# A two-layer encoder trunk on one core: weights and low parts ahead of copies and squares in the first unit, head-norm fans in pairs, and one value ahead of two maxima

## The reference, cut to what matters

```
x = x + 0.5 * swiglu(rmsnorm(x), w_gate, w_up, w_down)      # 1024 -> 2816 -> 1024
h = rmsnorm(x)
layer 0:  z = h @ w_in                       # u, g, q, k, v and 8 forget logits
          a = silu(rmsnorm(conv31(u * sigmoid(g)) + b))     # depthwise, 31 taps
          q, k = rmsnorm per head of 64; o = softmax(q k^T / 8 + decay, causal) @ v
          x = x + concat(a, o) @ w_out
layer 1:  x = x + (gate_b * conv3(gate_c * hh)) @ w_out
x = x + 0.5 * swiglu(rmsnorm(x), ...)
```

## Time and profile before

| | us |
|---|---|
| median of 3 runs | 1849.33 (1849.28 to 1849.39) |
| the profiled execution, its own time | 1849.31 |
| its span in the trace | 1847.5 |
| TensorE busy | 1835.4 |
| VectorE busy | 824.3 |
| ScalarE busy | 633.2 |
| GpSimd busy | 356.7 |

### The profile page before, as it was taken

How to read it: one execution, slowest core, us unless ns; L and a number is a source line. 1 busy time by engine, 2 the same in 40 slices (tenths; PEclk the granted TensorE clock), 3 DMA queues, 4 the chain that set the end, 5 groups by cost and what they waited for, 6 DMA issues and landing times.

```text
span 1847.5 us, 22267 instructions
## 1 busy us (share of the span) xinstructions
PE 1835.4 (99%) x8269; PEld 1504.5 (81%) x8269; DVE 824.3 (45%) x934; ACT 633.2 (34%) x833; POOL 356.7 (19%) x295
## 2 busy tenths in 40 slices
PE   8999999999999999999999999999999999999999
PEld 7888888888668888888888888888888888888887
DVE  6343433368856443443344343333455544343321
ACT  5333322247765333332233333222212333333221
POOL 5111111129853111111111111011213221111000
PEclk9999999999999999999999999999999999999999
DMA  5333343233104333333323333432333333333331
GB/s 162 103 91 102 91 125 94 77 80 92 35 24 126 101 93 98 95 114 105 88 79 95 99 93 100 121 94 81 92 91 103 91 102 92 102 91 110 108 111 35
DMA packets 341403, 174.85 MB, mean 95 GB/s; under 512 B 6304, under 2 KB 340332, under 8 KB 341356
## 3 DMA queue, kind: packets, MB, share of 16 engines
q1 hardware_dynamic: 337100, 172.12, 32.2%
q10 hardware_dynamic: 4256, 2.11, 0.4%
HBM read 172.10 MB, written 2.10 MB: 94 GB/s over the span
## 4 chain that ended last, share of the span: by engine, by line
PE 93%; DVE 4%; ACT 2%; issue 1%; POOL 0%; ACTq 0%; DVEq 0%; POOLq 0%
PE bank L1324 30%; PE bank L1326 30%; PE bank L1325 30%; DVE w_lo L964 1%; DVE conv L1000 1%; ACT w_hi L645 1%; ACT tap_prod L804 0%; PE bank L1530 0%; DVE neg_max L1180 0%; PE bank L1546 0%; ACT probs_a L857 0%; PE bank L1465 0%; DVE k_n L1129 0%; PE bank L1515 0%; DVE q_n L1129 0%
## 5 line engine op out<-in xcount | busy, mean ns | idle before, releaser
L964 DVE TENSOR_TENSOR w_lo<-raw,w_hi 128x1024 fp32r<-128x1024 f32 (+2 forms) x308 | 408.5, 1327 | 697.0 <-ACT w_hi L645 696.5
L1324 PE MATMUL bank<-xg_hi,w_hi 128*128 128x512 f32 x1728 | 673.8, 390 | 2.7 <-DVE w_lo L964 2.6
L1326 PE MATMUL bank<-xg_hi,w_lo 128*128 128x512 f32 x1728 | 672.3, 389 | 0.0
L1325 PE MATMUL bank<-xg_lo,w_hi 128*128 128x512 f32 x1728 | 672.3, 389 | 0.0
L645 ACT ACTIVATE w_hi<-raw 128x1024 fp32r<-128x1024 f32 (+2 forms) x308 | 339.9, 1104 | 775.6 <-PE bank L1326 775.5
L1324 PEld LDWEIGHTS bank<-xg_hi,w_hi 128*128 128x128 f32 x1728 | 324.3, 188 | 72.7 <-DVE w_lo L964 3.1
L1326 PEld LDWEIGHTS bank<-xg_hi,w_lo 128*128 128x128 f32 x1728 | 324.3, 188 | 67.6
L1325 PEld LDWEIGHTS bank<-xg_lo,w_hi 128*128 128x128 f32 x1728 | 324.4, 188 | 66.9 <-issue 0.2
L545 POOL TENSOR_TENSOR scaled<-acted,rstd 128x512 f32<-128x512 f32 x92 | 118.8, 1291 | 835.9 <-ACT acted L722 787.9
L1324 PE MATMUL bank<-h_hi,w_hi 128*128 128x512 f32 x704 | 274.5, 390 | 0.0
L1326 PE MATMUL bank<-h_hi,w_lo 128*128 128x512 f32 x704 | 274.0, 389 | 0.0
(11 more groups left out here) (193 smaller groups left out, 991.9 us busy)
## 6 DMA issues: line engine op xcount, KB each, us to landing
raw<-in_ffn_w_gate SPq DMA_DIRECT2D x88, 512.0 KB, 3.8
raw<-in_ffn_w_up SPq DMA_DIRECT2D x88, 512.0 KB, 3.8
raw<-in_ffn_w_down SPq DMA_DIRECT2D x64, 704.0 KB, 4.5
raw<-in_od_w_in SPq DMA_DIRECT2D x24, 512.0 KB, 3.7
raw<-in_ev_w_in SPq DMA_DIRECT2D x20, 512.0 KB, 3.8
raw<-in_ev_w_out SPq DMA_DIRECT2D x16, 256.0 KB, 2.8
raw<-in_od_w_out SPq DMA_DIRECT2D x8, 512.0 KB, 3.9
x_rows<-in_x SPq DMA_DIRECT2D x4, 512.0 KB, 6.7
```

The source lines that it names most:

```text
L964: dve.tensor_tensor(w_lo[:, u % 2, c0:c0 + n], raw[:, u % 4, 0:n], raws(w_hi[:, u % 2, c0:c0 + n]), ALU.subtract).then_inc(wlo_ready, 1)
L1324: pe.matmul(dst, a[0], b[0], start=start, stop=False)
L1325: pe.matmul(dst, a[0], b[1], start=False, stop=False)
L1326: return pe.matmul(dst, a[1], b[0], start=False, stop=stop)
```

## The change

Three things. In the first unit VectorE makes the low parts of tiles 0 and 1 and the low part of the weights before it copies the tiles, and tiles are copied in the order 0, 1, 2, 5, 6, 7, 3, 4. ScalarE makes the high part of the weights ahead of the first square, and six of the eight squares follow the second weights. The sum over partitions moves from the end of unit 1 into the middle of unit 2, and units 1 to 3 wait for the copies out of their banks. In the phase `v` the four fans stand in two pairs. On VectorE the taps around them are dealt out otherwise, four go into the attention steps 3 to 6, and the last value stands ahead of the maxima of step 1.

```diff
+    COPIES = [0, 1, 2, 5, 6, 7, 3, 4]
-    TAPS_V, TAPS_T = [2, 2, 2, 2, 2, 3, 4], 0
+    TAPS_V, TAPS_T = [2, 2, 3, 3, 3], 1
-    QK_FANS, V_SUMS, V_FANS = {6: 0, 7: 2}, (0, 0), [(1, 2), (1, 3), (2, 0), (2, 1)]
+    QK_FANS, V_SUMS, V_FANS = {6: 0, 7: 2}, (0, 0), {(1, 2): AB, (2, 0): AB + 2}
...
+            def first_square(n):
+                act.wait_ge(x_new, n + 1)
+                if n >= 2:
+                    act.wait_ge(sq_added, n - 1)
+                act.activation(sq[:, n % 2, :], x[:, COPIES[n], :], ACT.Square).then_inc(sq_ready, 1)
...
             for j in (0, 1):
                 first_high(j)
+            split_hi(phases[0], 0, 0)
             first_square(0)
-            split_hi(phases[0], 0, 0)
             for j in (2, 3):
                 first_high(j)
+            first_square(1)
             for j in range(4, KD):
-                first_square(j - 3)
                 first_high(j)
             split_hi(phases[0], 0, 1)
-            for j in (KD - 3, KD - 2, KD - 1):
+            for j in range(2, KD):
                 first_square(j)
...
                 qk_scale(4)
+                qk_scale(5)
                 conv_taps(TAPS_V[2])
-                qk_scale(5)
-                conv_taps(TAPS_V[3])
                 split_lo(ph, 0, 3)
                 qk_scale(6)
-                conv_taps(TAPS_V[4])
                 qk_scale(7)
-                conv_taps(TAPS_V[5])
+                conv_taps(TAPS_V[3])
...
                         value(1)
-                        conv_taps(TAPS_V[6])
+                        conv_taps(TAPS_V[4])
+                        value(3)
                         maxima(1)
-                        value(3)
...
-                    if t >= 2:
+                    if t >= 3:
                         conv_taps(TAPS_T, late=t >= LAST_IN_BANK)
...
             for j in (0, 1):
                 first_low(j)
+            split_lo(phases[0], 0, 0)
+            for j in (0, 1):
                 first_copy(j)
-            split_lo(phases[0], 0, 0)
-            for j in range(2, KD):
+            for j in (2, 3):
                 first_low(j)
-                if 3 <= j < KD - 1:
-                    first_copy(j - 1)
+            first_copy(2)
+            for j in range(4, KD):
+                first_low(j)
+            first_copy(3)
             split_lo(phases[0], 0, 1)
-            for j in (KD - 2, KD - 1):
-                first_copy(j)
+            for n in range(4, KD):
+                first_copy(n)
...
+                        if first and ph is phases[0] and u:
+                            pe.wait_ge(x_new, u + 3)
+                        if first and ph is phases[0] and u in (0, 2):
+                            hook = late_squares if u else turn_in
                         projection(ph, g, u, wait_x=first and u == 0, before=hook)
...
                         if first and u == 1 and ph is phases[0]:
-                            sum_squares(ph)
...
+            def late_squares(k):
+                if k == KD // 2:
+                    sum_squares(phases[0])
...
                             elif (u, tb) in V_FANS:
-                                fan(AB + V_FANS.index((u, tb)))
+                                fan(V_FANS[u, tb])
+                                fan(V_FANS[u, tb] + 1)
```

More of the change, by code:

```diff
@@ L663, in first_high @@
                                scale=vec[:, j + GAIN_COL[0]:j + GAIN_COL[0] + 1]).then_inc(xhi_ready, 1)
-            def first_square(j):
-                act.wait_ge(x_new, j + 1)
-                if j >= 2:
-                    act.wait_ge(sq_added, j - 1)
-                act.activation(sq[:, j % 2, :], x[:, j, :], ACT.Square).then_inc(sq_ready, 1)
+            def first_square(n):
[3 more added lines that the diff above has]
+                act.activation(sq[:, n % 2, :], x[:, COPIES[n], :], ACT.Square).then_inc(sq_ready, 1)
             logs = [0]
@@ L1240, in first_low, with first_copy @@
                                          ALU.mult, ALU.subtract).then_inc(xlo_ready, 1)
-            def first_copy(j):
+            def first_copy(n):
+                j = COPIES[n]
                 dve.tensor_copy(x[:, j, :], bank[TURN_BANKS[j % len(TURN_BANKS)]][:, :]).then_inc(x_new, 1)
@@ L1360, in group @@
                         hook = None
-                        if first and ph is phases[0] and u == 0:
-                            hook = turn_in
+                        if first and ph is phases[0] and u:
+                            pe.wait_ge(x_new, u + 3)
+                        if first and ph is phases[0] and u in (0, 2):
+                            hook = late_squares if u else turn_in
                         projection(ph, g, u, wait_x=first and u == 0, before=hook)
```

## The result

The changed kernel takes **1852.65 us** (median of 15 runs, 1851.31 to 1853.82); beside it on the same chip the kernel before takes 1849.32 us (15 runs, 1849.27 to 1849.39). The ratio is 1.0018, 95% interval 1.0011 to 1.0025: 3.3 us slower. The forecast was 1850.6 with a range up to 1852.6, so it missed by 2.05 us and the median lies just outside the range.

What follows compares the result with a forecast made beforehand. TensorE was taken as the bound, busy 1835.4 of 1847.5 us at full clock. First units +2.2 and attention -0.9 gave +1.3 us on the 1849.33 median: 1850.6 us, range 1848.5 to 1852.6.

Steps and rivals of the forecast that it cites:

- The gain of the first unit: First units: TensorE's first product at 9.8 instead of 11.38, unit 1 at 18.4 against 19.83, 1.4 us ahead.
- The stand at unit 2: Unit 2: squares paced by GpSimd's adds hold the third `w_hi`; TensorE stands 3.0 us, starting at 27.05 against 26.35.
- The rest of the first units at full clock: Units 2 to 5: later sum makes the fifth `w_lo` late, waits 0.45 and 0.2 us; first units +2.2 us.
- the bounds given: First units: the +2.2 us term could lie between +0.8 and +2.7 us.
- rival (c): Unit 2: the 3.0 us stand drops TensorE's clock to half; 1852.6, or 1854 if twice as long; 12 in 100.
- a clock under full behind the stand: After the stand at unit 2: a granted clock under full would show the forecast wrong.
- the wait for the odd probabilities: Attention near 500: TensorE waits about 1.4 us for the odd probabilities.
- GpSimd's bound on the turn: First attention turn: GpSimd scales the odd head until 501.62, so third scores start at 502.2 against 503.09, -0.9 us.
- Attention at full clock: Attention input: scores start about 1.8 us earlier, but only -0.9 us is kept; range 0 to -2.2.
- the taps moved into steps 3 to 6: Attention steps 3 to 6: four taps cost TensorE nothing if they fit VectorE's waits; otherwise the gain is 0.2.
- The fans: Attention input: a pair takes 0.43 us like a lone fan, so pairing saves 0.86 us.
- The sum: Whole kernel: first units +2.2 and attention -0.9 make +1.3 us, forecast 1850.6 us.

Runs made afterwards that it cites:

- e4: Changed kernel with ten filler matmuls that nothing reads on TensorE ahead of unit 2; 1852.18 us.
- e1: Changed kernel with the attention input put back as before, so only the first units changed; 1853.03 us.
- e3: Changed kernel with ScalarE making unit 2's high weights after four squares instead of eight; 1851.56 us.
- e2: Changed kernel with the first units put back as before, so only the attention input changed; 1849.67 us.
- e5: e2 with six filler matmuls between the even and odd half of the first attention turn; 1848.75 us.
- e9: e6 with VectorE's tap of step 6 moved ahead of the last value copy; 1848.26 us.
- e6: e2 with two more of GpSimd's tap adds moved behind the first scalings of odd heads; 1848.71 us.
- e11: Kernel before with only the four last fans of the head norms issued in two pairs; 1849.34 us.
- e8: e7 with GpSimd freed as in e6, the third square before the last high part, unit 2's weights after six squares; 1847.85 us.
- e10: e8 with the tap of step 6 moved ahead of the last value copy as in e9; 1847.40 us.
- e12: First-units part of the change alone, with three mends (third square earlier, unit 2's high weights before last two squares, selectors later); 1848.47 us.
- e7: e3 with GpSimd building its selectors behind the first phase's gates instead of ahead of them; 1849.79 us.

## Why the prediction was right and wrong

**The gain of the first unit: right.** First product 9.80 for 9.8, unit 1 at 18.35 for 18.4.

**The stand at unit 2: right**, place, cause and size: 27.08 for 27.05, six squares behind the second `w_hi` paced by adds, last square at 24.10 for 24.2, stand 2.86 us for 3.0 (27.05 less 23.95 is 3.1). One of the two meetings of an add and a `w_lo` held the squares, the other none of what unit 2 needs.

**The rest of the first units at full clock: nearly right.** e4 shows it without the fall at unit 2: the fifth `w_lo` was to be ready at 39.4 (by the forecast's own terms 30.8 + 9.64 - 0.9 it is 39.5) and TensorE to wait 0.45; TensorE starts at 39.50 after 0.35. The term was +2.2 us; e1's lower group gives +2.6, within the bounds given. The missing 0.4 comes a little at a time: e4's units 4, 5 and 6 start at 39.50, 45.21 and 50.79, against 37.34, 42.78 and 48.22 before, which is 2.16, 2.43 and 2.57 us behind, and the forecast had 2.0 at unit 4 and 2.2 from unit 5 on.

**The clock: the step that failed.** I had this fall as rival (c), with its mechanism, place and price, and gave it 12 in 100. I reasoned that "the longest stand inside the rows of before is 1.70 us, and no slice shows less than the full 2.4 GHz", which says nothing of a stand of 3.0 us; and the slices could not have shown a fall, since the changed kernel's, with two falls, show the same forty 9s. So the sum held nothing for the clock, and a clock under full behind the stand, which I had named as a sign of being wrong, came. By e1's groups the fall happened in 8 of its 11 runs. Rival (c)'s 1852.6 is the measured median to 0.05 us by luck: it put 2 us for one fall on top of 1850.6, while the median run, with a mean clock of 0.999, lost about 1.2 us by one fall and 0.8 us more than forecast in order. A fall costs less than I worked out for two reasons. Half rate lasted 3.4 us (28.3 to 31.7) and not 4; the start of the kernel, from which I took the 4 us, shows 1.00 in the clock column although its turns took twice as long, so it was no measured fall of the clock. And of the 1.7 us of lost work not all arrives. The sum of squares starts at 31.30 instead of e4's 29.92, 1.38 us late, and `mean_sq` behind it at 32.57 instead of 30.98, 1.59 late; but the fifth `w_lo` takes 1.54 us instead of e4's 1.89, and unit 4, which waits for it in both, starts 1.24 us late. e3 shows the other case: its three upper runs lie 1.7 us over the middle ones, the whole of the lost work.

**The second fall: missed.** I forecast the wait for the odd probabilities, about 1.4 us, and put nothing for it beyond GpSimd's bound on the turn. It is a 1.87 us stand, only 0.17 us more than the 1.70 us of the earlier trace rows behind which the profiled run of the kernel before shows full clock, and it drops the clock in 7 of e2's 11 runs. The 0.45 us that it is longer are a mis-sized term: a lone fan costs TensorE more than the 0.43 us to the next product, because the steps ahead of it and behind that product are longer too, 0.31 and 0.34 us for 0.23. TensorE's timeline before:

```profile
482.19 0.39 PE L1326 MATMUL bank<-w_hi,xg_lo 128*128 128x512 f32 x1
482.50 0.50 PE L1585 MATMUL bank<-head_rows,fan_rows 4*128 4x512 f32 x1
482.93 0.50 PE L1324 MATMUL bank<-w_hi,xg_hi 128*128 128x512 f32 x1
483.27 0.39 PE L1325 MATMUL bank<-w_lo,xg_hi 128*128 128x512 f32 x1
```

Two fans fewer to stand alone gave 1.3 us and not 0.86: e2's first scores start at 490.65, without a wait, where TensorE would have come at 491.97 before and at 491.1 by the forecast.

The Trainium skill, "TensorE: Matmul & The Clock Gate", section "Why this matters for your kernels", warns of gaps over about 3 us; for the first stand (2.86) the measurement is about at that edge, and for stands of 1.87 and 1.90 us it goes further than the page: behind them the clock fell too, in 7 of 11 and 3 of 11 runs. Where the two differ, the measurement decides.

**Attention at full clock: right in kind, too large.** Forecast -0.9, measured -0.5. The third scores of e5 start at 502.30 for the forecast 502.2: that lead was there, and still is at the ninth (516.22 for 517.02). It is lost at turn 6 (tenth scores 519.28 for 519.21), and 0.5 us of it comes back at the turn near 524, where the kernel before waits 0.45 us. The step that failed reads that the taps moved into steps 3 to 6 "cost nothing on TensorE as long as they fit in waits that VectorE has there", with 0.2 as the gain if one does not. One does not, the one in step 6; e9 moves it and gets 0.5 us more. I had looked at VectorE's room as a sum and not at step 6, where a weight split stands. That the price was 1.66 us on the maximum and not the tap's own 0.7 comes from two neighbours made longer (1.45 for 0.67, 1.17 for 0.69) when shifted: in e6 GpSimd's square starts at 513.67, ahead of the `w_lo` (513.80), in e9 at 513.64, behind it (513.15). By the Trainium skill, "SBUF — State Buffer", section "SBUF: two separate sides", the one that starts first holds the shared ports; the trace agrees (1.45 against 0.67). Durations of this kind, 2.18 for 1.22, I had used at the first units and not here.

**The fans: right in kind and worth nothing alone.** 0.43 us for a pair, but more saved by it than forecast, as above; e11 shows no gain in time, because the last `k_n` bounds the scores.

**The sum.** Forecast +2.2 - 0.9 = +1.3. Measured at full clock +2.6 - 0.5 = +2.1, with the clock's falls +3.3 in the median. So 0.8 us of the miss are sizes (0.4 in the first units, 0.4 in attention) and 1.2 us are the clock. In which of the three groups the median of 15 runs lies is chance; from the 1.000 group alone the forecast is 0.7 us off.

**What stays open.** Why a fall comes in one run and not in the next of the same kernel. The run's mean clock says that it did, nothing in the profile of one run says why. Why the fall at unit 5 of e3 costs 1.7 us rests on its groups and one profile. e4's run of 1854.2 us and the two high runs of e5 are not explained. Whether the stand of 1.70 us can drop the clock too is only hinted at: of the 113 timed runs of the kernel before 7 took 1850.16 to 1850.30 us, 0.9 over the rest, all with a mean clock of 0.999, but 7 runs at the usual time show 0.999 too. The 55 runs of e6, e8, e9, e10 and e12 have none like them; of these only e6 and e9 keep that stand (1.25 and 1.72 us in their profiles), and at 7 in 113 their 22 runs would show one or two, so that they show none says little. None of the seven was profiled.

## What to carry to other kernels

When a change moves a wait, ask what the longest stand of TensorE will be afterwards, not only whether the sum of waits grows: a stand that is hidden in the order of work can still cost 0.9 to 1.7 us by the clock behind it, and slices of 46 us don't show it. Work that is slipped between critical instructions of a helper engine must be placed by its neighbours: 0.70 us of tap cost the next maximum 1.66 us, because it pushed a `w_lo` and a scaling into GpSimd's adds. And list every item behind which a needed split now stands, on the engine it is issued from: the mends here only put squares, one `w_hi` and the selectors in another place, and turned +2.6 us into -0.9.

## What the runs showed of the hardware

- In the profiled runs the granted clock fell to half behind stands of TensorE of 2.86 us (changed kernel, 28.3 to 31.7), 2.84 (e1, 27.6 to 31.0), 1.87 (changed kernel, 506.2 to 509.6; e2, 502.3 to 505.7) and 1.90 (e3, 45.1 to 48.5), each time only 0.5 to 1.2 us after work had begun again, and stayed there for 3.4 us. The profiled run of the kernel before has no fall behind its 1.70 us stand, nor has that of e7 behind its 1.87.
- By the groups of run times the fall does not come in each run: at the 2.84 us stand in 8 of e1's 11 runs, at the 1.87 us stand in 7 of 11 in e2 and e7 each, at the 1.90 us stand in 3 of e3's 11. This makes groups 0.7 to 1.7 us apart where the usual runs of the kernel before agree within 0.2 us, so a median of few runs of such a kernel can be off by 1 us. In the changed kernel the run's mean granted clock, in its third decimal, tells the groups apart; elsewhere it mostly does (one of e1's three lower runs shows 0.999).
- With fillers that nothing reads in the stand the clock stayed full (e4's profiled run from 28 to 32, and by their times 9 of e5's 11 runs), at no price.
- The same eight selects on GpSimd took 3.36 us in the changed kernel (28.64), where VectorE stood until 32.57, 4.26 in e4, where it worked from 30.98 on, and 5.45 in e3 (28.22), where it worked from 28.88 on.
